# Nesting nine conditional blocks and halving the squares of a final norm, in a one-core encoder trunk with a mixture of experts

## The reference, cut to what matters

```python
def rmsnorm(x, g):
    x32 = x.astype(jnp.float32)
    y = x32 * lax.rsqrt(jnp.mean(x32 * x32, axis=-1, keepdims=True) + EPS)
    return (y * g.astype(jnp.float32)).astype(x.dtype)
...
    def run_block(args):
        xb, e = args
        return (jax.nn.silu(xb @ w_eg[e]) * (xb @ w_eu[e])) @ w_ed[e]
...
        h = h + mix
        h = h + hier_moe(rmsnorm(h, lp['g_ffn']), ...)
...
    return rmsnorm(h, g_final), new_states
```

## Time and profile before, and how to read it

| | us |
|---|---|
| median of three executions | 1290.44 |
| lowest, highest | 1290.29, 1292.85 |
| the profiled execution, its own time | 1289.0 |
| its span (first to last event on the core) | 1287.1 |
| PE busy in the span | 1140.2 |
| DVE, ACT, POOL busy in the span | 522.9, 387.3, 185.0 |

### The profile page before, as it was taken

The page is one execution under the profiler, slowest core; times in us unless marked ns, Lnnn a source line. Parts: engine busy times, 40 slices in busy tenths (PEclk is TensorE's granted clock), DMA queues, the critical chain, the costliest instruction groups (busy, mean ns, idle before and its releaser), DMA issues.

```text
span 1287.1 us, 16996 instructions
## 1 busy us (share of the span) xinstructions
PE 1140.2 (89%) x6759; PEld 808.4 (63%) x6759; DVE 522.9 (41%) x923; ACT 387.3 (30%) x599; POOL 185.0 (14%) x197
## 2 busy tenths in 40 slices
PE   4899799999999999999999479999999999999942
PEld 3898677787888899999999443333343333333311
DVE  6131577663246555534331622333333433333314
ACT  5312666666556444343321101101011000000102
POOL 7000011110304446422200000000000000000000
PEclk7999899999999999999998769999999999999976
DMA  8364433342212212253360479999999999999902
GB/s 177 58 104 85 79 49 50 50 50 36 64 51 81 67 50 66 75 140 97 98 235 23 185 308 426 429 426 428 427 428 428 428 427 427 429 425 429 382 5 74
DMA packets 96398, 266.89 MB, mean 207 GB/s; under 512 B 4156, under 2 KB 77080, under 8 KB 84040
## 3 DMA queue, kind: packets, MB, share of 16 engines
q1 hardware_dynamic: 89088, 248.00, 54.7%
q0 software_dynamic: 3456, 10.25, 2.1%
q10 hardware_dynamic: 3784, 7.65, 1.7%
HBM read 258.24 MB, written 7.64 MB: 207 GB/s over the span
## 4 chain that ended last, share of the span: by engine, by line
PE 56%; DMA 26%; DVE 8%; ACT 5%; issue 4%; SPq 0%; POOL 0%; ACTq 0%; DVEq 0%; POOLq 0%
DMA arena<-in_w_expert_up 22%; PE za L1068 11%; PE pj L718 10%; PE pj L720 9%; PE pj L719 9%; DMA ring<-in_w_in 3%; PE pj L745 2%; PE zb L1088 2%; DVE arena L1655 1%; DVE arena L1654 1%; PE zb L843 1%; PE ms L1001 1%; ACT arena L1278 1%; PE zb L841 1%; ACT arena L1280 1%
## 5 line engine op out<-in xcount | busy, mean ns | idle before, releaser
L1068 PE MATMUL za<-arena 128*64 128x512 f32 x1024 | 237.7, 620 | 22.8 <-DMA arena<-in_w_expert_up 21.9
L718 PE MATMUL pj<-u_high_r,ring_r 128*128 128x288 f32 x768 | 237.2, 309 | 9.9 <-DVE ring_r L1538 4.8
L719 PE MATMUL pj<-u_rest_r,ring_r 128*128 128x288 f32 x768 | 227.8, 297 | 0.0
L720 PE MATMUL pj<-u_high_r,ring_r 128*128 128x288 f32 x768 | 227.7, 297 | 0.0
L1068 PEld LDWEIGHTS za<-arena 128*64 128x64 f32 x1024 | 74.1, 142 | 178.2 <-issue 143.6
L718 PEld LDWEIGHTS pj<-u_high_r,ring_r 128*128 128x128 f32 x768 | 145.9, 190 | 17.9 <-issue 10.9
L719 PEld LDWEIGHTS pj<-u_rest_r,ring_r 128*128 128x128 f32 x768 | 146.1, 190 | 2.2 <-issue 1.0
L720 PEld LDWEIGHTS pj<-u_high_r,ring_r 128*128 128x128 f32 x768 | 145.7, 190 | 0.0
L1538 DVE TENSOR_TENSOR ring_r<-ring,ring_r 128x1024 fp32r<-128x1024 f32 x68 | 85.6, 1266 | 123.8 <-ACT ring_r L1166 123.7
L1088 PE MATMUL zb<-arena 128*64 128x512 f32 x512 | 113.4, 595 | 4.1 <-DVE arena L1991 3.4
L1088 PEld LDWEIGHTS zb<-arena 128*64 128x64 f32 x512 | 35.9, 137 | 74.6 <-issue 73.3
(11 more groups left out here) (423 smaller groups left out, 2037.7 us busy)
## 6 DMA issues: line engine op xcount, KB each, us to landing
arena<-in_w_expert_gate SPq DMA_DIRECT2D x32, 2048.0 KB, 17.0
arena<-in_w_expert_up SPq DMA_DIRECT2D x32, 2048.0 KB, 17.5
arena<-in_w_expert_down SPq DMA_DIRECT2D x32, 2048.0 KB, 18.4
ring<-in_w_in SPq DMA_DIRECT2D x32, 512.0 KB, 8.5
ring<-in_w_gate SPq DMA_DIRECT2D x24, 512.0 KB, 4.1
arena<-in_x_prompt SPq DMA_DIRECT2D x8, 512.0 KB, 6.6
ring<-in_w_branch_out SPq DMA_DIRECT2D x8, 512.0 KB, 3.3
arena<-in_w_branch_out SPq DMA_DIRECT2D x4, 512.0 KB, 3.4
```

The lines of the kernel that those rows point to most:

```text
L718: pe.matmul(out, left[0], right[0], start=k == 0, stop=False)
L719: pe.matmul(out, left[0], right[1], start=False, stop=False)
L720: return pe.matmul(out, left[1], right[0], start=False, stop=k == last - 1)
L1068: m = pe.matmul(za[j * BLK:(j + 1) * BLK, b, :], xT[:, k, j * BLK:(j + 1) * BLK], w[:, j * KD + k, :], start=k == 0, stop=k == KD - 1)
```

## The change

- On all five engines the nine conditional blocks are nested: block `j + 1` stands inside block `j`, and all nine end at the same place. `more` is an `ExitStack` that is left after the loop.
- ACT's `final(t)` is split. `final_square(q, t)` squares one half of 512 columns and sums it into `ss3[q, t]`; five left halves come first, then per tile the right half and `final_root(t)`. DVE's `final_half(t)` makes the left sum a mean plus EPS, and the root takes `sqrt(right sum / D + that)`, with the addition in ACT's scale and bias.
- Ahead of these, ACT takes a root of one column of `ones`, whose result nobody reads.
- The five stores are issued by SP in place of ACT, after SP's conditional blocks.

```diff
-        square = [at(wexp_off + 16384 + D * i, D) for i in range(2)]
+        square = [at(wexp_off + 16384 + 512 * i, 512) for i in range(2 * NT)]
...
-        ss3 = tiny(8)
+        ss3 = tiny(2, NT)
...
-            for j in range(OPAIRS):
-                with sp.If(total > j):
+            with ExitStack() as more:
+                for j in range(OPAIRS):
+                    more.enter_context(sp.If(total > j))
...
+            for t, (o0, n) in enumerate(TT):
+                sp.wait_ge(S["fin_r"], t + 1)
+                dst = o["y_p"][0, o0:o0 + n, :] if t < NT - 1 else o["y_s"][0]
+                sp.dma_start(dst, h[0:n, t, :]).then_inc(S["fin_out"], 16)
...
-            for j in range(OPAIRS):
-                with pe.If(total > j):
+            with ExitStack() as more:
+                for j in range(OPAIRS):
+                    more.enter_context(pe.If(total > j))
                     expert_pair(EPAIRS + j, ((EPAIRS + j) % 2, (EPAIRS + j) // 2), over=j)
                     scatter_over(j)
             scatter(EPAIRS - 1, range(2 * NT))
...
-            def final(t):
-                o0, n = TT[t]
-                act.wait_ge(S["sc_r"], 2 * NT * (EPAIRS - 1) + NT + t + 1)
-                act.activation(square[t % 2][0:n, :], h[0:n, t, :], ACT.Square, accum_out=ss3[0:n, t:t + 1]
-                               ).then_inc(S["ssq_r"], 1)
+            def final_square(q, t):
+                n = TT[t][1]
+                act.wait_ge(S["sc_r"], 2 * NT * (EPAIRS - 1) + NT * q + t + 1)
+                act.activation(square[NT * q + t][0:n, :], h[0:n, t, q * 512:(q + 1) * 512], ACT.Square,
+                               accum_out=ss3[0:n, q, t:t + 1]).then_inc(S["ssq_r"], 1)
+
+            def final_root(t):
+                n = TT[t][1]
+                act.wait_ge(S["ssq_r"], 3 * NT + t + 1)
                 act.wait_ge(S["var_r"], 2 * NT + t + 1)
-                act.activation(rs3[0:n, t:t + 1], ss3[0:n, t:t + 1], ACT.Sqrt).then_inc(S["std_r"], 1)
-                act.wait_ge(S["fin_r"], t + 1)
-                dst = o["y_p"][0, o0:o0 + n, :] if t < NT - 1 else o["y_s"][0]
-                act.dma_start(dst, h[0:n, t, :]).then_inc(S["fin_out"], 16)
+                act.activation(rs3[0:n, t:t + 1], ss3[0:n, 1, t:t + 1], ACT.Sqrt, scale=1.0 / D,
+                               bias=ss3[0:n, 0, t:t + 1]).then_inc(S["std_r"], 1)
...
+            act.activation(rs3[:, NT:NT + 1], ones[:, 0:1], ACT.Sqrt)
             for t in range(NT):
-                final(t)
+                final_square(0, t)
+            for t in range(NT):
+                final_square(1, t)
+                final_root(t)
...
+            def final_half(t):
+                n = TT[t][1]
+                dve.wait_ge(S["ssq_r"], 2 * NT + t + 1)
+                dve.tensor_scalar(ss3[0:n, 0, t:t + 1], ss3[0:n, 0, t:t + 1], 1.0 / D, EPS, ALU.mult, ALU.add
+                                  ).then_inc(S["var_r"], 1)
+
             def final_norm(t):
                 n = TT[t][1]
                 hv = h[0:n, t, :]
-                dve.wait_ge(S["ssq_r"], 2 * NT + t + 1)
-                dve.tensor_scalar(ss3[0:n, t:t + 1], ss3[0:n, t:t + 1], 1.0 / D, EPS, ALU.mult, ALU.add
-                                  ).then_inc(S["var_r"], 1)
...
             add(EPAIRS - 1, range(NT))
             for t in range(NT):
                 add(EPAIRS - 1, (NT + t,))
+                final_half(t)
                 if t > 0:
                     final_norm(t - 1)
             final_norm(NT - 1)
```

More of the change, by code:

```diff
@@ L1485, in _ @@
             total = act.value_load(over_total[0:1, 0:1], min_val=0, max_val=OVB)
-            for j in range(OPAIRS):
-                with act.If(total > j):
+            with ExitStack() as more:
+                for j in range(OPAIRS):
+                    more.enter_context(act.If(total > j))
                     expert_pair(EPAIRS + j, ((EPAIRS + j) % 2, (EPAIRS + j) // 2), over=j)
+            act.activation(rs3[:, NT:NT + 1], ones[:, 0:1], ACT.Sqrt)
             for t in range(NT):
-                final(t)
+                final_square(0, t)
+            for t in range(NT):
+                final_square(1, t)
+                final_root(t)
         def bc(v, *shape):
@@ L2079, in _ @@
             total = dve.value_load(over_total[0:1, 0:1], min_val=0, max_val=OVB)
-            for j in range(OPAIRS):
-                with dve.If(total > j):
+            with ExitStack() as more:
+                for j in range(OPAIRS):
+                    more.enter_context(dve.If(total > j))
                     expert_pair(EPAIRS + j, ((EPAIRS + j) % 2, (EPAIRS + j) // 2), over=j)
@@ L2309, in _ @@
             total = pool.value_load(over_total[0:1, 0:1], min_val=0, max_val=OVB)
-            for j in range(OPAIRS):
-                with pool.If(total > j):
+            with ExitStack() as more:
+                for j in range(OPAIRS):
+                    more.enter_context(pool.If(total > j))
                     expert_pair(EPAIRS + j, ((EPAIRS + j) % 2, (EPAIRS + j) // 2))
```

## The result

The changed kernel takes 1259.06 us (median of four, 1258.0 to 1260.32), beside 1291.64 us for the kernel before (median of four): a ratio of 0.9753, 95% interval 0.9735 to 0.9772. The forecast was 1261.0 us in a range of 1258 to 1269. The profiled execution took 1258.18 us, its span is 1256.1 us, 31.0 less than before.

A forecast was written before the change was run, and what follows sets the result against it. PE bound 89% of the span, then a 21.42 us gap of PE code fetches, then an ACT-DVE ring. -21.75 - 8.1 + 0.3 = -29.5 us took 1289.0 to 1259.5; plus 1.44 for the median, 1261.0, range 1258 to 1269.

The forecast's parts named there:

- the 21.42 us: Empty stretch between pair 15's end and PE's first scatter product, read as nine PE jumps each waiting a 3.19 us fetch.
- R1: Rival: code arrives as one ordered stream, so the gap stays and only the last stage gains; 1282.6 us, chance 0.08.
- R3: Rival: the long jump empties the code store, 13 blocks come in, PE resumes at 1274.5; 1297.6 us, chance 0.02.
- R2: Rival: the gap is the count's reading, the wait ahead or nine block ends, not jumps; 1281.7 us, chance 0.05.
- Nesting, PE: At the skipped blocks, eight of nine PE jumps go; one long jump remains, PE resuming at 1237, between 1236.6 and 1240.6.
- the nearest row: Last code fetch before PE resumed in the kernel before: 1.7 to 2.6 us from fetch to PE's first weight load.
- Nesting, DVE: After the last `y_rest`, 0.9 us for count and jump; first add at 1239.0 in place of 1260.75, -21.75 us.
- ACT's root of `ones`: Moves ACT's 1.28 us table load ahead of the final norm's squares, into time where ACT waits for adds.
- Halves and the last stage: Final norm with ten half squares: DVE becomes the bound at 2.23 us a tile, 14.9 in place of 23.0, -8.1 us.
- Stores: At the end, SP issues the five stores; the last may wait for its predecessor, 0 to 1.1 us, taken as +0.3.
- The sum: Nesting -21.75, last stage -8.1 and stores +0.3 make -29.5 us: 1259.5 profiled, forecast 1261.0.
- The rule on control flow: Skill's 108 ns per compare-and-branch would save eight, 0.9 us, at the skipped blocks; the forecast set it aside.

The follow-up runs named there:

- short blocks: Changed kernel, but nine blocks one after another on all engines and PE's cut to the scatter products; 1256.14 us, ratio 0.975 to the kernel before.
- three groups: Changed kernel, but the nine blocks nested in three groups of three on all engines; 1268.51 us, ratio 0.9829 to the kernel before.

## Why the prediction was right

**What bounds.** The reading of the 21.42 us was right: PE's jumps, each waiting for code. PE's jump records and the short blocks show it, and nested PE alone shows that no other engine had a share in the gap. One count was off: not nine jumps waited but eight, since the first took 0.35 us, and the ninth transfer starts after PE has landed. The sum doesn't use that count. R1, code as one ordered stream, falls with the two transfers of the changed kernel; so does R3. R2 falls with the jump records and the short blocks; PE's reading of the count is over by 1233.2, ahead of the gap:

```profile
L1135 PEldq SEQ_ASSERT  x1: 32/32/32, 1233.1 to 1233.1; - x1
```

**Nesting, PE.** I took one fetch, hidden behind the last products, and PE resuming at 1237: it was 1236.86. The transfer came at about 1234, as the first of nine had. From it to PE's first product are about 2.9 us, more than the 1.7 to 2.6 of the nearest row: the long jump takes 3.74 where the eight took about 3.1. The 1237 came out because it stood near the upper end of what the row gave, and there is some luck in that. What I gave as the price of a second fetch, 3.2, was too low in one respect: a far jump straight after a landing costs 4.6 to 5.1. The change has no such jump.

**Nesting, DVE.** First add forecast at 1239.0, measured 1238.83, -21.92 us in place of -21.75. The 0.9 us that I took for the count and the jump were 1.02: about 0.3 of the reading, whose rest is hidden behind `y_rest`, and about 0.6 from the jump on.

**ACT's root of `ones`.** As forecast: the load runs from 1237.76, ahead of the first square at 1239.55, and is worth 1.28.

**Halves and the last stage.** -9.13 us in place of -8.1. The mechanism was right, DVE is the bound after the first tile; three terms were a little too large. A tile takes DVE 2.05, not 2.23: I put mean and reciprocal in a row, 0.18 and 0.19, but the reciprocal belongs to the tile before, starts 0.07 after the mean and runs beside it (1245.70 and 1245.77). Three tiles are 0.5 less. The first product ended 6.35 after the first add, not 6.7, since ACT's squares follow each other at 0.62 rather than 0.7. And the last tile followed after 1.38, not 1.5.

**Stores.** +0.05 in place of +0.3: 3.39 us from the last product to the span's end, 3.34 before. The short distance to the store ahead cost next to nothing.

**The sum.** -31.0 against -29.5 by the profiled executions; of the 1.5 the last stage is 1.0 (9.13 less 8.1), the stores 0.25 and the first add 0.17 (21.92 less 21.75). By the medians it is 1259.06 against 1261.0.

**The rule on control flow.** The Trainium skill, "Advanced Engine Details and Errata", section Control Flow Timing, gives about 108 ns for a compare-and-branch. The 0.19 us from one of DVE's nine jumps to the next and the 0.20 to 0.33 of PE's past short blocks are two to three times that; PE's 3 to 5 us are another thing. The Trainium skill, "Runtime: NRT & Kernel Launch", section Instruction fetch mechanics, names that thing, the fetch of the target page of a taken branch. The trace agrees: the one long jump brings its target, and none of the blocks between.

## What to carry to other kernels

A conditional block that is skipped still costs whatever it takes to get past its code. Look for a stretch where every engine is empty and only a queue of the kind "instruction" moves, and look up the jumps of that engine by their source line, whose records give the price of each; the transfers alone can mislead by one or more, as here nine stood for eight stops and, with three groups, six for three. Nest such blocks, so that one jump leaves them all, or keep them short, or put the one long jump where the engine still has products in hand. And in a ring of small steps over two engines, take out the step that only waits to issue a store.

## What the runs showed of the hardware that was not expected

- PE reads its instructions well ahead of its array. In the changed kernel the jump past the blocks starts at 1233.0, with 3.3 us of products still to run (until 1236.29), which hid most of its 3.74; with short blocks all nine jumps are over at about 1231.8, ahead of the end of the products at 1232.66.
- After a landing PE fetches the following block unasked (the change's second transfer). A far jump taken at once after a landing took 4.67 to 5.09 us, one far jump from the loop 3.74, and a jump to the next block, already on its way by this reading, about 3.1 (the eight). Three groups of three are therefore nearly half as bad as nine blocks in a row, 10.73 against 22.95.
- On DVE, reading a count and one jump past all nine blocks take 1.5 us from 1237.2 to 1238.8, of which 1.02 show as a wait because the rest runs beside `y_rest`.
